# Inverting a triangular block with 32-wide instead of 64-wide tile products in a DeltaNet mixer

## The chip, the cores and the metric

The kernel runs on one core of one Trainium2 chip. The metric is the device time of one launch in microseconds (us), as the median of several runs. A core has five engines: TensorE (PE, matrix products; its weight loads are listed apart as PEld), VectorE (DVE), ScalarE (ACT), GpSimd (POOL) and SyncE (SP, which only issues transfers here). PE writes to the accumulation memory PSUM (8 banks of 128 partitions x 512 float32), the others take it from there.

## The reference, cut to what matters

One inference step of a two-layer backbone. Each layer has a mixer (windowed attention beside a bidirectional gated DeltaNet) and a routed mixture of experts. The change is in the DeltaNet's triangular solve:

```
a_mat = where(strict, einsum('bhnik,bhnjk->bhnij', kb, k) * decay, 0.0)
sol = triangular_solve(a_mat + eye(CHUNK), rhs, left_side=True, lower=True, unit_diagonal=True)
u0, w = sol[..., :DV], sol[..., DV:]
qk = where(causal, einsum('bhnik,bhnjk->bhnij', q, k) * decay, 0.0)
def step(S, xs):
    u = u0_c - einsum('bhck,bhkv->bhcv', w_c, S)
    o = einsum('bhck,bhkv->bhcv', qd_c, S) + einsum('bhij,bhjv->bhiv', qk_c, u)
    S = S * gt_c[..., None, None] + einsum('bhck,bhcv->bhkv', kd_c, u)
```

The kernel solves by an explicit inverse of `I + a_mat`, in chunks of 128 tokens. All of it is float32.

## The kernel before

The program has straight-line phases for each of two layers: projection, mixer, tail, experts, combine. Only the mixer phase (`mixer_phase`) changes. It runs 5 steps `s`, one per tile of 128 tokens, and in each step both directions `d` (0 forward, 1 backward) for 4 heads `h`. Every engine has its own instruction list, written out by hand; engines meet by semaphores alone, so the order within each list is the order of the code. Four attention pieces (`n0` to `n0 + 3`) are threaded between the DeltaNet's parts of a step: `next_scores` (PE: values of the piece before, then scores), `stats` (DVE: maximum), `exps` (ACT), `norm` (DVE), `turn` (PE: transposes), `take` (ACT: copy out of PSUM).

A step goes:

1. `g_p`, `r_p`: products K K^T and the decay exponents; ACT makes `E` (L1161), DVE makes `Bt` (two 64-wide diagonal blocks per 128, L1234) and `BtL` (the corner that joins them, L1236).
2. POOL masks `Bt` for each level into `NTb` (L964), DVE makes the first approximation `Y` (L1240), PE transposes it to `X` (L1052, copied by ACT L1168).
3. Five levels `v` (block sizes 2, 4, 8, 16, 32 are joined to pairs). In each, for both directions: `T1 = NTb^T X` (PE), a copy to SBUF (ACT, L1172), then `Y^T T1` and `T1^T Y` (PE), and DVE subtracts them from `X` (L1252) and `Y` (L1259). One product of all heads is `eight`: 8 matmuls with 64x64 tiles. In float32 each matmul is issued as two passes, and each pass is a weight load and a matmul record, so one `eight` is 32 PE records.
4. The last join of the two 64-blocks: `t1l` (L1104), ACT copies (L1179), `yl` (L1117), DVE copies into the inverse `YF` (L1274). Between them PE runs `ks`, and after them `turn(n0 + 1)` (L1022) and `qs` (L1045).
5. `z` on DVE (L1278, L1279), `next_scores(n0 + 2)` (L1034, L1001), then the solve `xz`, `u2`, state update, outputs and the last attention piece.

SP issues three small transfers at the mixer's start, and in layer 0 a fourth of 12.8 MB that fills `y_table` with zeros.

## Time and profile before

| | us |
|---|---|
| median of 3 runs (lowest, highest) | 2103.43 (2102.64, 2104.16) |
| the profiled execution's own time | 2101.1 |
| its span, first to last instruction | 2099.4 |
| PE / DVE / ACT / POOL busy | 1760.4 / 1294.8 / 958.4 / 211.8 |

The span is what the profiler saw of one execution. Busy time is a union over instructions of one engine; idle time in front of an instruction is listed with what released it. "issue" is idle time for which the profile shows no releaser. Times in a timeline count from the span's start. The mixer phase of layer 0 lies at 290 to 542 us, that of layer 1 at 1332 to 1573 us.

### The profile page before, as it was taken

The page shows a single profiled execution, that of the slowest core. Times are in us where ns is not written, and L with a number is a line of the kernel's source. Part 1 is how long each engine was busy: PE and PEld are TensorE (multiplying, and loading weights), DVE is VectorE, ACT ScalarE, POOL GpSimd, SP SyncE. Part 2 cuts the span into 40 slices and gives each one's busy share as a digit, 9 for nine tenths or more (in the row PEclk, how much of TensorE's full clock was granted, in tenths as well). Part 3 has the DMA queues.
Part 4 walks back from the last instruction along what each step waited for, and adds up shares of the span by engine and source line. Part 5 has one row for each costly group of instructions (what it writes and reads, how often), then busy time and mean ns, then how long its engine had stood idle before and what let it go on. Part 6 is the DMA issues. An engine that isn't in the chain of part 4 may idle for free. (4 is left out here: it accounts for less than half of the span.)

```text
span 2099.4 us, 38037 instructions
## 1 busy us (share of the span) xinstructions
PE 1760.4 (84%) x14245; PEld 1412.2 (67%) x14246; DVE 1294.8 (62%) x1877; ACT 958.4 (46%) x1486; POOL 211.8 (10%) x267
## 2 busy tenths in 40 slices
PE   5499978999698399999954999899987939999991
PEld 0299767888444188888843997788873538888881
DVE  0439635666443488696646495576662469999664
ACT  0134533343311288686633445343332238888641
POOL 0000022222000000000010000222220010000002
PEclk8699999999798599999986999999997969999995
DMA  9532043000557499798833220000004069999744
GB/s 393 238 110 79 5 147 128 3 2 2 172 218 274 192 387 399 283 392 339 300 144 111 87 83 1 13 12 2 3 2 143 31 228 389 407 397 397 311 171 180
DMA packets 96326, 376.48 MB, mean 179 GB/s; under 512 B 14478, under 2 KB 35030, under 8 KB 65478
## 3 DMA queue, kind: packets, MB, share of 16 engines
q1 hardware_dynamic: 80486, 316.76, 40.2%
q0 software_dynamic: 8496, 30.94, 3.9%
q10 hardware_dynamic: 7216, 26.97, 3.2%
q8 instruction: 94, 1.54, 0.3%
q14 instruction: 34, 0.28, 0.0%
HBM read 332.86 MB, written 41.78 MB: 178 GB/s over the span
## 5 line engine op out<-in xcount | busy, mean ns | idle before, releaser
L1926 DVE TENSOR_TENSOR expert_w_lo<-shared,expert_w_hi 128x2048 fp32r<-128x2048 f32 x192 | 430.5, 2284 | 44.0 <-ACT expert_w_hi L1868 42.9
L1868 ACT ACTIVATE expert_w_hi<-shared 128x2048 fp32r<-128x2048 f32 x192 | 361.3, 1916 | 56.2 <-PEq L142 52.0
L1810 PE MATMUL ps<-expert_w_hi,expert_x_hi 128*128 128x512 f32 x592 | 232.6, 393 | 5.1 <-DVE expert_x_lo L1922 5.1
L1812 PE MATMUL ps<-expert_w_hi,expert_x_lo 128*128 128x512 f32 x592 | 232.4, 393 | 0.0
L1811 PE MATMUL ps<-expert_w_lo,expert_x_hi 128*128 128x512 f32 x592 | 232.2, 392 | 0.0
L1810 PEld LDWEIGHTS ps<-expert_w_hi,expert_x_hi 128*128 128x128 f32 x592 | 112.4, 190 | 29.4 <-issue 5.9
L1811 PEld LDWEIGHTS ps<-expert_w_lo,expert_x_hi 128*128 128x128 f32 x592 | 112.3, 190 | 23.5
L1812 PEld LDWEIGHTS ps<-expert_w_hi,expert_x_lo 128*128 128x128 f32 x592 | 112.3, 190 | 23.5
L1846 PE MATMUL ps<-expert_w_hi,expert_hid_hi 128*128 128x512 f32 x296 | 118.6, 401 | 1.2 <-ACT expert_hid_hi L1900 0.5
L1847 PE MATMUL ps<-expert_w_lo,expert_hid_hi 128*128 128x512 f32 x296 | 115.6, 391 | 0.0
L964 POOL TENSOR_TENSOR mixer_NTb<-mixer_Bt,consts_sb 128x256 f32<-128x256 f32 x120 | 89.2, 767 | 229.2 <-DVE mixer_Bt L1234 181.1
L1409 PE MATMUL ps<-shared,attT 128*128 128x512 f32 x160 | 76.4, 625 | 28.9 <-DMA shared<-in_w_out 28.9
L603 PE MATMUL ps<-projection_hT_hi,kvrows_r 128*128 128x256 f32 (+1 forms) x384 | 90.3, 317 | 5.9 <-DVE shared_r L511 5.9
L1852 PE MATMUL ps<-expert_w_hi,expert_hid_lo 128*128 128x512 f32 x296 | 91.2, 389 | 0.0
L1252 DVE TENSOR_TENSOR mixer_X<-mixer_X,ps 128x256 f32<-128x256 f32 x100 | 42.2, 422 | 78.3 <-PE ps L1052 76.0
L607 PE MATMUL ps<-projection_hT_hi,shared_r 128*128 128x256 f32 (+1 forms) x384 | 88.6, 313 | 0.0
L565 PE MATMUL ps<-shared_r,projection_hT_hi 128*128 128x512 f32 (+1 forms) x240 | 88.2, 367 | 0.0
L771 DVE SCALAR_TENSOR_TENSOR shared<-shared,projection_cwT 128x644 f32<-128x644 f32 x96 | 85.2, 888 | 2.5
L1796 PE MATMUL ps<-consts_sb,expert_xg 128*128 128x128 f32 x312 | 54.9, 282 | 36.5 <-DMA expert_xg<-h_table,expert_cur_idx 36.5
L1172 ACT ACTIVATE mixer_T<-ps 128x256 f32<-128x256 f32 x100 | 38.4, 384 | 102.0 <-PE ps L1052 98.0
L1409 PEld LDWEIGHTS ps<-shared,attT 128*128 128x128 f32 x160 | 31.8, 201 | 68.9 <-issue 39.0
L1776 POOL COPY expert_cur_idx<-slot_tokens 128x1 int32 (+1 forms) x39 | 10.5, 270 | 647.9 <-PE ps L1796 588.8
(344 smaller groups left out, 3710.7 us busy)
## 6 DMA issues: line engine op xcount, KB each, us to landing
shared<-in_w_gate SPq DMA_DIRECT2D x64, 1024.0 KB, 6.8
shared<-in_w_up SPq DMA_DIRECT2D x64, 1024.0 KB, 8.6
shared<-in_w_down SPq DMA_DIRECT2D x64, 1024.0 KB, 18.8
setup_m_ada_ring<-in_w_ada SPq DMA_DIRECT2D x24, 1024.0 KB, 10.6
shared<-in_w_in SPq DMA_DIRECT2D x10, 2048.0 KB, 8.0
y_table<-expert_y ACTq DMA_DIRECT2D x37, 512.0 KB, 8.8
y_table<-zero SPq DMA_DIRECT2D x1, 12800.0 KB, 41.1
qkv<-in_w_ada SPq DMA_DIRECT2D x11, 1024.0 KB, 5.1
```

What stands on the lines that cost most here:

```text
L603: pe.matmul(out, w_hi[:, k, :], h_hi[:, k, t * P:until * P], start=(k == 0), stop=False)
L607: mm = pe.matmul(out, w_lo[:, k, :], h_hi[:, k, t * P:until * P], start=False, stop=(k == KD - 1))
L964: return pool.tensor_tensor(NTb[:, slot, d], Bt[:, d], row(G.c(f"level{level}_{d}"), DH), ALU.mult)
L1409: mm = pe.matmul(G.ps[:, BO + r % NOB, :], src[:, t * P:(t + 1) * P], wo[:, k, h * 512:(h + 1) * 512], start=(k == 0), stop=(k == KD - 1))
L1810: pe.matmul(bank, hi, w_hi[:, j, w], start=first, stop=False)
L1811: pe.matmul(bank, hi, w_lo[:, j, w], start=False, stop=False)
L1812: return pe.matmul(bank, lo, w_hi[:, j, w], start=False, stop=last)
L1846: pe.matmul(G.ps[:, 5 + h, :], h_hi[:, at], w_hi[:, j, w], start=(q == 0), stop=False)
L1847: pe.matmul(G.ps[:, 5 + h, :], h_hi[:, at], w_lo[:, j, w], start=False, stop=False)
L1852: mm = pe.matmul(G.ps[:, 5 + h, :], h_lo[:, at], w_hi[:, j, w], start=False, stop=(q == KF - 1))
L1868: act.activation(w_hi[:, j, :], raw[:, j, :], ACT.Copy).then_inc(w_hi_done, 1)
L1926: dve.tensor_tensor(w_lo[:, j, :], raw[:, j, :], w_hi[:, j, :].bitcast(F32), ALU.subtract).then_inc(w_lo_done, 1)
```

## The change

The blocks that the levels work on become 32 wide: four 32x32 diagonal tiles per head stand in a packed tile of 32 columns, `XY` holds `X` and `Y` side by side, and one product of all heads is `strips`, 16 matmuls with 32x32 tiles (64 PE records). `Bt` is kept whole (128 wide, one DVE instruction per direction), and the level's mask is no longer put on it by POOL: the product is made with the unmasked tile, and DVE multiplies the mask in when it copies `T1` out of PSUM. The first approximation is made by PE (`first_p`, four `strips`) and DVE. There are four levels. The join of 32-blocks to 64-blocks (`t2_p`, `merge_p`, `x64_done`, `y64_done`) and that of 64-blocks to the whole make only the corner block; ACT puts the pieces into `X64` and `YF`, DVE copies the diagonal into `YF`. `turn(n0 + 1)` and `next_scores` move behind both `qs`, `norm(n0 + 1)` behind `z`, `stats(n0 + 1)` behind the levels.

```diff
-LEVELS = [2, 4, 8, 16, 32]
+HB, QB = 64, 32
+LEVELS = [2, 4, 8, 16]
...
-        Bt, BtL = ph.sb("Bt", [P, 2, DH, HB]), ph.sb("BtL", [P, DH, HB])
...
+        Bt = ph.sb("Bt", [P, 2, DH, P])
+        XY = ph.sb("XY", [P, 2, 2, DH, QB])
+        T1 = ph.sb("T1", [P, 2, DH, QB])
+        X64 = ph.sb("X64", [P, DH, HB])
         T1L = ph.sb("T1L", [P, DH, HB])
-        NTb = ph.sb("NTb", [P, 2, 2, DH, HB])
...
-                def masked(slot, d, level):
-                    return pool.tensor_tensor(NTb[:, slot, d], Bt[:, d], row(G.c(f"level{level}_{d}"), DH), ALU.mult)
...
-                    for v in range(LV):
-                        for d in range(2):
...
-                            masked(v % 2, d, LEVELS[v]).then_inc(s_["nt_done"], 1)
...
-                def eight(b, c, lhsT, rhs, sem):
+                def strips(b, c, lhsT, rhs):
 
                     for h in range(DH):
-                        for r in range(2):
-                            mm = pe.matmul(G.ps[half(r), b, 256 * c + h * HB:256 * c + (h + 1) * HB],
-                                           lhsT(h)[half(r)], rhs(h)[half(r)], start=True, stop=True)
-                    mm.then_inc(s_[sem], 1)
+                        for q in range(4):
+                            mm = pe.matmul(G.ps[quarter(q), b, c + h * QB:c + (h + 1) * QB], lhsT(h, q), rhs(h, q), start=True, stop=True)
+                    return mm
...
+                    eye = lambda h, q: G.c("eye")[quarter(q)]
+                    for d in range(2):
+                        pe.wait_ge(s_["bt_done"], at(s, d))
+                        own = lambda h, q: Bt[quarter(q), d, h, quarter(q)]
+                        strips(d, 0, own, eye)
+                        strips(d, 128, eye, own).then_inc(s_["first_p"], 1)
+                    for d in range(2):
                         four(2 + d, kT[d], qT[d], "kq_p")
                     next_scores(n0)
-                    for d in range(2):
-                        pe.wait_ge(s_["y0_done"], at(s, d))
-                        eight(d, 0, lambda h: Y[:, d, h, :], lambda h: G.c("eye"), "x0_p")
                     for v in range(LV):
                         for d in range(2):
...
-                            eight(d, 0, lambda h: NTb[:, v % 2, d, h, :], lambda h: X[:, d, h, :], "t1_p")
+                            pe.wait_ge(s_["xy_done"], xy_at(s, v - 1, d))
+                            strips(d, 256, lambda h, q: Bt[quarter(q), d, h, quarter(q)],
+                                   lambda h, q: XY[quarter(q), d, 0, h, :]).then_inc(s_["t1_p"], 1)
                         if v == 2:
                             turn(n0)
                         if v == 3:
                             next_scores(n0 + 1)
                         for d in range(2):
                             pe.wait_ge(s_["t1_done"], lev(s, v, d))
...
-                            eight(d, 1, lambda h: Y[:, d, h, :], lambda h: T1[:, d, h, :], "xx_p")
-                            eight(2 + d, 0, lambda h: T1[:, d, h, :], lambda h: Y[:, d, h, :], "yy_p")
...
+                            y = lambda h, q: XY[quarter(q), d, 1, h, :]
+                            t1 = lambda h, q: T1[quarter(q), d, h, :]
+                            strips(d, 0, y, t1)
+                            strips(d, 128, t1, y).then_inc(s_["xy_p"], 1)
+                    for d in range(2):
+                        pe.wait_ge(s_["xy_done"], xy_at(s, LV - 1, d))
+                        for h in range(DH):
+                            for b in range(2):
+                                q1, q2 = halves_of(d, b)
+                                mm = pe.matmul(G.ps[quarter(q2), d, 256 + h * QB:256 + (h + 1) * QB], Bt[quarter(q1), d, h, quarter(q2)],
+                                               XY[quarter(q1), d, 0, h, :], start=True, stop=True)
+                        mm.then_inc(s_["t2_p"], 1)
+                    for d in range(2):
+                        pe.wait_ge(s_["t2_done"], at(s, d))
+                        for h in range(DH):
+                            q1, q2 = halves_of(d, d)
+                            pe.matmul(G.ps[quarter(q2), d, h * QB:(h + 1) * QB], XY[quarter(q2), d, 1, h, :], T1[quarter(q2), d, h, :],
+                                      start=True, stop=True)
+                            for b in range(2):
+                                q1, q2 = halves_of(d, b)
+                                mm = pe.matmul(G.ps[quarter(q1), d, 128 + h * QB:128 + (h + 1) * QB], T1[quarter(q2), d, h, :],
+                                               XY[quarter(q2), d, 1, h, :], start=True, stop=True)
+                        mm.then_inc(s_["merge_p"], 1)
+                    for d in range(2):
+                        pe.wait_ge(s_["qk_done"], at(s, d))
+                        pe.wait_ge(s_["x64_done"], at(s, d))
                     for h in range(DH):
                         for d in range(2):
-                            mm = pe.matmul(G.ps[half(1 - d), 2, h * HB:(h + 1) * HB], BtL[half(d), h, :],
-                                           X[half(d), d, h, :], start=True, stop=True)
+                            mm = pe.matmul(G.ps[half(1 - d), 2, h * HB:(h + 1) * HB], Bt[half(d), d, h, half(1 - d)],
+                                           X64[half(d), h, :], start=True, stop=True)
...
                     for d in range(2):
+                        pe.wait_ge(s_["y64_done"], at(s, d))
...
                     pe.wait_ge(s_["t1l_done"], s + 1)
...
-                    turn(n0 + 1)
                     four(2, qT[0], lambda h: S[:, st, 0, h, :], "qs_p")
                     pe.wait_ge(s_["yo_done"], s + 1)
                     four(3, qT[1], lambda h: S[:, st, 1, h, :], "qs_p")
+                    turn(n0 + 1)
...
+                    exps(n0)
+                    take(n0)
+                    for d in range(2):
+                        act.wait_ge(s_["t2_p"], at(s, d))
+                        act.activation(T1[:, d], t1_of(d), ACT.Copy).then_inc(s_["t2_done"], 1)
+                    for d in range(2):
+                        for q in (2 * d, 2 * d + 1):
...
+                            act.activation(X64[quarter(q), :, quarter(q % 2)], XY[quarter(q), d, 0], ACT.Copy)
+                    for d in range(2):
+                        act.wait_ge(s_["merge_p"], at(s, d))
+                        q1, q2 = halves_of(d, d)
+                        act.activation(X64[quarter(q2), :, quarter(q1 % 2)], pair_of(d)[quarter(q2), 0], ACT.Copy,
+                                       scale=-1.0).then_inc(s_["x64_done"], 1)
+                    for d in range(2):
+                        for b in range(2):
+                            q1, q2 = halves_of(d, b)
+                            ins = act.activation(YF[quarter(q1), d, :, quarter(q2)], pair_of(d)[quarter(q1), 1], ACT.Copy, scale=-1.0)
+                        ins.then_inc(s_["y64_done"], 1)
                     act.wait_ge(s_["t1l_p"], s + 1)
                     act.activation(flat(T1L[:, :, :]), G.ps[:, 2, 0:256], ACT.Copy, scale=-1.0).then_inc(s_["t1l_done"], 1)
-                    take(n0 + 1)
+                    exps(n0 + 1)
                     for d in range(2):
...
+                    take(n0 + 1)
...
-                        for b in range(2):
-                            ins = dve.tensor_tensor(Bt[half(b), d], bank(2 + d)[half(b), :, half(b)], E[half(b), d, :, half(b)], ALU.mult)
-                        ins.then_inc(s_["b_done"], 1)
...
-                    for d in range(2):
-                        dve.wait_ge(s_["n1_done"], at(s, d))
-                        dve.tensor_tensor(Y[:, d], NTb[:, 1, d], row(G.c("eye"), DH), ALU.add).then_inc(s_["y0_done"], 1)
+                        dve.tensor_tensor(Bt[:, d], bank(2 + d), E[:, d], ALU.mult).then_inc(s_["bt_done"], 1)
+                    for d in range(2):
+                        first = G.c(f"first_{d}").rearrange("p (a n) -> p a n", a=2).unsqueeze(2).to_broadcast([P, 2, DH, QB])
+                        dve.wait_ge(s_["first_p"], at(s, d))
+                        dve.tensor_tensor(XY[:, d], pair_of(d), first, ALU.mult).then_inc(s_["first_done"], 1)
+                        dve.wait_ge(s_["first_done"], at(s, d))
+                        both = XY[:, d].rearrange("p a h n -> p (a h) n")
+                        dve.tensor_tensor(both, both, row(G.c("eye"), 2 * DH), ALU.add).then_inc(s_["xy_done"], 1)
                     for d in range(2):
                         dve.wait_ge(s_["kq_p"], at(s, d))
                         dve.tensor_tensor(QK[:, d], bank(2 + d), E[:, d], ALU.mult).then_inc(s_["qk_done"], 1)
                     stats(n0)
                     for v in range(LV):
                         for d in range(2):
-                            dve.wait_ge(s_["xx_p"], lev(s, v, d))
...
-                            dve.tensor_tensor(X[:, d], X[:, d], blocks(d, 1), ALU.subtract).then_inc(s_["x_done"], 1)
...
+                            dve.wait_ge(s_["t1_p"], lev(s, v, d))
+                            dve.tensor_tensor(T1[:, d], t1_of(d), row(G.c(f"level{LEVELS[v]}_{d}"), DH), ALU.mult).then_inc(s_["t1_done"], 1)
+                        for d in range(2):
+                            dve.wait_ge(s_["xy_p"], lev(s, v, d))
+                            dve.tensor_tensor(XY[:, d], XY[:, d], pair_of(d), ALU.subtract).then_inc(s_["xy_done"], 1)
                         if v == 1:
                             norm(n0)
-                        if v == 3:
-                            stats(n0 + 1)
-                    norm(n0 + 1)
...
+                    for d in range(2):
+                        dve.wait_ge(s_["xy_done"], xy_at(s, LV - 1, d))
+                        for q in range(4):
+                            ins = dve.tensor_copy(YF[quarter(q), d, :, quarter(q)], XY[quarter(q), d, 1])
+                        ins.then_inc(s_["diag_done"], 1)
+                    stats(n0 + 1)
...
+                    norm(n0 + 1)
```

How the rows stand, in the third step of layer 0. PE, from the second level's first product on; `mixer_T_0` is `T1`. Before:

```order
L1052 MATMUL ps<-mixer_X,mixer_NTb 64x64 x16
L1052 MATMUL ps<-mixer_T_0,mixer_Y 64x64 x8
L1052 MATMUL ps<-mixer_Y,mixer_T_0 64x64 x8
L1052 MATMUL ps<-mixer_T_0,mixer_Y 64x64 x8
L1052 MATMUL ps<-mixer_Y,mixer_T_0 64x64 x8
L1052 MATMUL ps<-mixer_X,mixer_NTb 64x64 x16
L1022 MATMUL ps<-consts_sb,shared 128x128 x8
```

and now:

```order
L1057 MATMUL ps<-mixer_XY,mixer_Bt 32x32 x32
L1057 MATMUL ps<-mixer_T_0,mixer_XY 32x32 x16
L1057 MATMUL ps<-mixer_XY,mixer_T_0 32x32 x16
L1057 MATMUL ps<-mixer_T_0,mixer_XY 32x32 x16
L1057 MATMUL ps<-mixer_XY,mixer_T_0 32x32 x16
L1057 MATMUL ps<-mixer_XY,mixer_Bt 32x32 x32
L1027 MATMUL ps<-consts_sb,shared 128x128 x8
```

Each product has twice the matmuls; the place of the transposes (`turn(n0)`) is the same.

PE from the corner's first product on, before:

```order
L1104 MATMUL ps<-mixer_X,mixer_BtL 64x64 x8
L1045 MATMUL ps<-shared,qkvT 128x128 x8
L1117 MATMUL ps<-shared,mixer_T1L 64x64 x8
L1022 MATMUL ps<-consts_sb,shared 128x128 x8
L1045 MATMUL ps<-shared,qkvT 128x128 x8
L1034 MATMUL ps<-shared,qkv 64x128 x6
L1034 MATMUL ps<-shared,mixer_vctx 64x128 x2
```

and now:

```order
L1125 MATMUL ps<-mixer_X_0,mixer_Bt 64x64 x8
L1050 MATMUL ps<-shared,qkvT 128x128 x8
L1139 MATMUL ps<-shared,mixer_T1L 64x64 x8
L1050 MATMUL ps<-shared,qkvT 128x128 x8
L1027 MATMUL ps<-consts_sb,shared 128x128 x8
L1039 MATMUL ps<-shared,qkv 64x128 x6
L1039 MATMUL ps<-shared,mixer_vctx 64x128 x2
```

The transposes of piece `n0 + 1` stand directly ahead of the values that need them.

DVE from the last subtraction of a level on, before (L1221 to L1224 are `norm(n0 + 1)`, L1278 and L1279 make `z`):

```order
L1264 TENSOR_TENSOR shared<-mixer_Y,ps 64x4x64 x2
L1221 TENSOR_TENSOR mixer_rden<-mixer_rsum,mixer_es 128x2
L1222 RECIPROCAL mixer_rden<-mixer_rden 128x2
L1224 TENSOR_SCALAR shared<-shared,mixer_rden 128x512 x2
L1274 COPY shared<-ps 64x4x64 x2
L1278 TENSOR_TENSOR shared<-ps,dn_ecum 128x512
L1279 TENSOR_TENSOR shared<-kvrows,shared 128x512
L1278 TENSOR_TENSOR shared<-ps,dn_ecum 128x512
L1279 TENSOR_TENSOR shared<-kvrows,shared 128x512
```

and now (L1252 to L1255 are `norm(n0 + 1)`):

```order
L1247 TENSOR_TENSOR mixer_sx<-mixer_nm,mixer_sink 128x2
L1295 COPY shared<-ps 64x4x64 x2
L1299 TENSOR_TENSOR shared<-ps,dn_ecum 128x512
L1300 TENSOR_TENSOR shared<-kvrows,shared 128x512
L1299 TENSOR_TENSOR shared<-ps,dn_ecum 128x512
L1300 TENSOR_TENSOR shared<-kvrows,shared 128x512
L1252 TENSOR_TENSOR mixer_rden<-mixer_rsum,mixer_es 128x2
L1253 RECIPROCAL mixer_rden<-mixer_rden 128x2
L1255 TENSOR_SCALAR shared<-shared,mixer_rden 128x512 x2
```

`norm(n0 + 1)` stood ahead of the copies into `YF` and now stands behind all of `z`.

## Rows read from the trace of the kernel before

**Rows 1.** The page: span, instruction fetch queue of PE (packets, MB, share), one transfer.

```profile
span 2099.4 us, 38037 instructions
...
q8 instruction: 94, 1.54, 0.3%
...
y_table<-zero SPq DMA_DIRECT2D x1, 12800.0 KB, 41.1
```

**Rows 2.** Busy time in both mixer phases: window, length, engines (x records), PEclk, DMA.

```profile
290.00:541.80 251.80, 220.13 (x3904) 197.40 (x3904) 163.46 (x379) 92.70 (x274) 64.09 (x77) 1.00 0.18 59
1331.50:1572.60 241.10, 219.29 (x3904) 196.93 (x3904) 162.23 (x377) 92.67 (x274) 64.06 (x77) 1.00 0.03 7
```

**Rows 3.** Timeline, third step of layer 0, one level: start, length, engine, line.

```profile
403.71 0.85 ACT L1172 ACTIVATE mixer_T<-ps 128x256 f32<-128x256 f32 x2 [0.75 <-PE ps L1052]
...
404.14 0.68 PE L1052 MATMUL ps<-mixer_T,mixer_Y 64*64 64x64 f32 x16
...
406.74 0.85 ACT L1172 ACTIVATE mixer_T<-ps 128x256 f32<-128x256 f32 x2 [2.18 <-PE ps L1052]
```

**Rows 4.** Timeline, the same step from `E` to the solve's first product.

```profile
391.45 2.25 ACT L1161 ACTIVATE shared<-ps,dn_bias 128x128 f32<-128x128 f32 x8 [0.24 <-PE ps L1070]
...
400.68 0.85 ACT L1172 ACTIVATE mixer_T<-ps 128x256 f32<-128x256 f32 x2 [0.40 <-PE ps L1052]
...
420.98 0.68 PE L1104 MATMUL ps<-mixer_X,mixer_BtL 64*64 64x64 f32 x16 [0.77 <-DVE mixer_X L1252]
...
422.11 0.88 DVE L1224 TENSOR_SCALAR shared<-shared,mixer_rden 128x512 f32<-128x512 f32 x2
...
423.57 0.68 PE L1117 MATMUL ps<-shared,mixer_T1L 64*64 64x64 f32 x16
424.18 0.85 PEld L1022 LDWEIGHTS ps<-consts_sb,shared 128*128 128x128 f32 x8
...
425.32 1.02 ACT L1154 ACTIVATE shared<-ps 128x1024 f32<-128x1024 f32 x1 [3.22 <-PE ps L1022]
...
429.27 1.86 PEld L1045 LDWEIGHTS ps<-shared 128*128 128x128 f32 x16
```

**Rows 5.** Timeline of PE, first step of layer 0, two of four idle gaps.

```profile
307.62 0.39 PE L1052 MATMUL ps<-mixer_X,mixer_NTb 64*64 64x64 f32 x6 [2.73 <-issue]
...
328.50 0.50 PE L1104 MATMUL ps<-mixer_X,mixer_BtL 64*64 64x64 f32 x9 [2.26 <-issue]
```

**Rows 6.** Windows from gap to gap there; columns as in rows 2.

```profile
307.60:314.50 6.90, 4.41 (x125) 4.02 (x126) 3.62 (x9) 1.54 (x4) 4.13 (x5) 1.00 1.06 357
314.50:321.30 6.80, 4.58 (x125) 4.14 (x125) 2.10 (x5) 0.77 (x2) 0.00 (x0) 1.00 1.05 351
```

**Rows 7.** Transfers: at 304.5 to 332 us, at 353.9 to 357.7 us, and the smallest.

```profile
q8 instruction: 4, 0.07, 0.9%
q8 instruction: 2, 0.03, 3.4%
mixer_sink<-in_sink SPq DMA_DIRECT2D x1, 4.0 KB, 2.2
```

**Rows 8.** DVE groups by form: busy, mean ns of one, idle before.

```profile
L1252 DVE TENSOR_TENSOR mixer_X<-mixer_X,ps 128x256 f32<-128x256 f32 x100 | 42.2, 422 | 78.3 <-PE ps L1052 76.0 <-issue 0.3
L1213 DVE TENSOR_REDUCE mixer_mx<-ps 128x2 f32<-128x1024 f32 x16 | 19.5, 1222 | 10.5 <-PE ps L1011 10.5
L1243 DVE TENSOR_TENSOR shared<-ps,shared 128x512 f32<-128x512 f32 x20 | 12.9, 686 | 0.3
L1202 DVE COPY attT<-ps 128x128 f32<-128x128 f32 x40 | 11.4, 285 | 10.9 <-PE ps L1034 10.4
```

**Rows 9.** The smallest matmuls, in layer 0's tail.

```profile
685.46 0.27 PE L1482 MATMUL ps<-ones_bf,tail_sel 128*16 128x1 bf16 x5 [6.88 <-DVE tail_sel L1660]
```

**Rows 10.** Setup, before and after PE's clock fell; columns as in rows 2.

```profile
19.70:23.00 3.30, 1.28 (x12) 0.16 (x8) 0.00 (x0) 0.00 (x0) 0.00 (x0) 1.00 1.01 422
23.00:29.80 6.80, 5.54 (x24) 0.60 (x24) 1.38 (x2) 0.00 (x0) 0.00 (x0) 0.50 1.01 419
```

More of the change, by code:

```diff
@@ L77, in constants, with joined @@
     parts = {"ident": j == i, "ones": np.ones((P, P)), "upper": j <= i, "lower": j >= i, "before": j < i}
-    ib = HB * (j // HB) + np.arange(HB)[None, :]
-    parts["eye"] = j == ib
-    for s in [1] + LEVELS:
-        sign = -1.0 if s == 1 else 1.0
-        same = (j // (2 * s)) == (ib // (2 * s))
-        parts[f"level{s}_0"] = sign * (same & (j % (2 * s) < s) & (ib % (2 * s) >= s))
-        parts[f"level{s}_1"] = sign * (same & (j % (2 * s) >= s) & (ib % (2 * s) < s))
+    iq = QB * (j // QB) + np.arange(QB)[None, :]
+    parts["eye"] = j == iq
+    def joined(s):
+        same = (j // (2 * s)) == (iq // (2 * s))
+        below = same & (j % (2 * s) >= s) & (iq % (2 * s) < s)
+        above = same & (j % (2 * s) < s) & (iq % (2 * s) >= s)
+        return below, above
+    below, above = joined(1)
+    parts["first_0"] = -1.0 * np.concatenate([below, above], axis=1)
+    parts["first_1"] = -1.0 * np.concatenate([above, below], axis=1)
+    for s in LEVELS:
+        parts[f"level{s}_0"], parts[f"level{s}_1"] = joined(s)
     parts["tokens"] = np.stack([np.broadcast_to(np.arange(NT)[None, :] * P, (P, NT)),
@@ L921, in at, with lev, xy_at, halves_of @@
             return 2 * s + d + 1
-        def lev(s, v, d, n=LV):
-            return 2 * (n * s + v) + d + 1
+        def lev(s, v, d):
+            return 2 * (LV * s + v) + d + 1
+        def xy_at(s, v, d):
+            return 2 * ((LV + 1) * s + v + 1) + d + 1
+        def halves_of(d, b):
+            return (2 * b, 2 * b + 1) if d == 0 else (2 * b + 1, 2 * b)
         def first_visit(s, d):
@@ L940, in mixer_phase @@
         half = lambda b: slice(HB * b, HB * (b + 1))
+        quarter = lambda q: slice(QB * q, QB * (q + 1))
+        pair_of = lambda d: G.ps[:, d, 0:256].rearrange("p (a h n) -> p a h n", a=2, h=DH)
+        t1_of = lambda d: G.ps[:, d, 256:384].rearrange("p (h n) -> p h n", h=DH)
         bank = lambda b: G.ps[:, b, :].rearrange("p (h n) -> p h n", h=DH)
@@ L1254, in _ @@
-                            if v:
-                                dve.wait_ge(s_["y_done"], lev(s, v - 1, d, LV - 1))
-                            else:
-                                dve.wait_ge(s_["y0_done"], at(s, d))
-                            if v < LV - 1:
-                                dve.tensor_tensor(Y[:, d], Y[:, d], blocks(2 + d), ALU.subtract).then_inc(s_["y_done"], 1)
-                            else:
-                                if s == 0:
-                                    dve.wait_ge(s_["yf_zero"], 1)
-                                for b in range(2):
-                                    ins = dve.tensor_tensor(YF[half(b), d, :, half(b)], Y[half(b), d], blocks(2 + d)[half(b)],
-                                                            ALU.subtract)
-                                ins.then_inc(s_["yf_done"], 1)
+                            dve.wait_ge(s_["t1_p"], lev(s, v, d))
```

51 lines of the change are left out of this document (8 added, 43 removed).

## The prediction

> **What bounds the kernel now.** I read the two mixer windows first: they take 251.8 and 241.1 us of the span of 2099.4, TensorE's clock is at its full level throughout (share 1.00, which is 2.4 GHz), PE is busy 220 of them, DVE 163, ACT 93, POOL 64 [rows 1, 2]. Nothing outside the mixers changes, so the question is ten steps (five per layer), about 50 us each. Then I followed the third step of layer 0 in the timeline. One level takes 3.03 us (the copies of `T1` start at 403.71 and 406.74) [rows 3]. The 16 passes of one `eight` take 0.68 us with the last one's latency of 0.22, so 0.46 without; six of these are 2.8 of the 3.03: inside the levels PE's products are the bound. From `E` (391.45) to the first copy of `T1` (400.68) it is 9.2 us, from there to the corner product 20.3 (420.98), from the second corner product `yl` (423.57) to the solve `xz` (429.27) 5.7 [rows 4]. Layer 0's first step has something else: PE stands idle until 307.62 and 328.50, the first and last of four such gaps, without a releaser [rows 5], and from one resumption to the next there are 125 or 126 matmuls and as many weight loads [rows 6]. With the semaphore instructions that is 256 records, and four packets of 16 KB were fetched in that time (4 for 27.5 us) [rows 7]: 16 KB is 256 instructions of 64 bytes. So PE's instructions come in blocks of 256, at most one block is fetched ahead, and while the 12.8 MB of zeros (41.1 us to landing) [rows 1] hold the queues at a DMA share of 1.06, one block takes 6.9 us [rows 6].
>
> **What the change does to the products.** An `eight` was 32 PE records, a `strips` is 64. Per step 32 `eight` (1,024 records) become 28 `strips` and two small joins (1,792 + 160 = 1,952): about 930 more on some 1,650. How long does a `strips` take? In an `eight` two tiles alternate and 16 passes take 0.46 us, 29 ns each, 58 ns per pass on one tile [rows 3]. With half the columns and four tiles, 32 passes take 8 x 29 = 0.23 us if tiles are independent; if each pass costs what tiny matmuls on one tile do ((0.27 - 0.165) / 4 = 26 ns [rows 9]; 0.165 is the latency of one), 0.83 us. I take 0.27: the existing products show tiles overlapping, and the 26 ns row uses a single tile.
>
> The Trainium skill ("TensorE: Matmul & The Clock Gate", Back-to-back issue gap) gives a floor of about 25 ns per matmul however small; the tiny row agrees. By that rule a `strips` would be 32 x 25 = 0.8 us; it is the second rival.
>
> **Levels without a supply limit.** One direction's chain: `t1` 0.27 + 0.2 latency, hand-over 0.05, DVE masks 128 columns (0.29, the 128-column copy from PSUM [rows 8]), hand-over 0.05, two `strips` 0.54 + 0.2, 0.05, DVE subtracts 256 columns 0.42 [rows 8], 0.05: 2.1 us per level against 3.03. The other direction fits in between. `norm(n0)` puts 1.4 on DVE ahead of the third level's masks, `turn(n0)` 0.9 on PE, the scores 2.3 in the fourth; in all 12.5 us for four levels. The join adds `t2`, ACT's copies and the merge. ACT's 128-column instructions follow each other every 0.28 us (8 in 2.25 [rows 4]), and eight of them (two `T1`, four diagonal copies, two corners) are in the chain: 2.5 us. The corner product starts 15.05 us after the first `T1` copy instead of 20.3.
>
> **Head.** `Bt` takes one DVE instruction of 0.69 [rows 8] instead of three of 0.42; four `strips` are done while `E`'s second half is made; the first masks of `T1` now stand on DVE behind `stats(n0)` (reduce 1.22 [rows 8], and 0.6 around it). The first copy comes at 400.95 instead of 400.68: +0.3. POOL's masks cost nothing before (hidden) and nothing after.
>
> **Supply.** From there the third step needs 1,640 records to the end of the merge, 6.4 blocks, and 384 per level, 1.5 blocks in 2.1 us: one per 1.4 us. How long is one block's fetch L without the zeros? The smallest transfer, 4 KB, lands after 2.2 us; a fetch of 16 KB runs in one packet of 1.07 us on average (0.3% of 16 x 2099 us for 94 packets) [rows 1, 7]. Below: 2.2. Above: 3.6, since two packets 3.6 us apart were followed by no idle time [rows 7]. I take 2.2 + 1.07 less the small transfer's own part of some 0.35 = 2.9. Walking the step: a block is entered at 401.25 and the next arrives L later, four times in a row, since their contents last less than L; then the scores (56 records in 2.3 us) space the next entry by 3.65; the last block waits L again; ACT's last copies add 1.1. The corner product stands at 401.25 + 4L + 3.65 + L + 1.1 = 406.0 + 5L = 420.5 for L = 2.9, against 420.98 before. Nearly all that the levels won is lost waiting for instructions: -0.5 (with the head in it).
>
> **Tail.** Before, `norm(n0 + 1)` ran at 422.11 beside `ks`, the transposes at 424.18, ACT's `take` at 425.32, the values from 427, `xz` at 429.27 [rows 4]. Now the norm stands behind the `YF` copies (0.86) and four `z` instructions (2.75). Counted from `yl`: 0.7 until it is out, 0.86, 2.75, norm 1.3, transposes to `take` 1.15, `take` 1.0, hand-over 0.1, values and scores 2.3: `xz` follows 10.15 us after `yl` instead of 5.7. The queue behind the waiting transposes is values, scores and the solve itself, for which the DeltaNet's own `z` has long been ready. +4.45 per step. In the first step of a layer the pieces are narrower and I take +3.5.
>
> **Layer 0's first step.** From the first products until 331.7, when the zeros have landed, blocks come every 6.9 to 7 us. The block boundary 165 records into the phase is passed at about 296.3, the next block is there at 304.5, then 311.5, 318.5, 325.4, 331.7; then L apart: 334.6, 337.5. The step needs about 2,090 records up to the end of the merge, which lies in the last of these: 338.4, corner product 339.3 instead of 328.5 [rows 5]. +10.8, and the tail's 3.5: +14.3.
>
> **Sum.** Nine steps x (-0.5 + 4.45) = +35.6, the first step +14.3: +50 us. On the profiled execution's own 2101.1 (span 2099.4 and 1.7 around it) that is 2151; the median of the runs is 2.3 above the profiled execution, so 2153.
>
> **Rivals.**
> - *Supply never binds without the zeros, or at all* (other side: faster). Place: the block boundaries in the levels. If L is under 1.4 us, the third step's corner comes at 416.0 (-5.0) and the tail gives back 4.45: -0.5 per step. If layer 0's first step is not held up either, 10 x -0.5 = -5: 2098. For it: in 9 of 10 steps the trace shows no such gap. Against: rows 5 and 6, and the 2.2 us of the smallest transfer. If only the first step is held, 9 x -0.5 + 13 = +8: 2111. What decides between faster and not is whether a block arrives in the 1.4 us in which its forerunner is used up.
> - *Passes are bound by issue*, 26 ns each: a level is six times 0.83 = 5.0 us, the four with norm, turn and scores some 23, the head +1.1; corner +4.6, tail +4.45, 9 us in ten steps: +90, 2193.
> - *The clock falls too.* In the setup PE was busy 1.28 of 3.3 us at share 1.00 and then stood at 0.50 (1.2 GHz) in the 6.8 us behind it [rows 10]. In the levels it would have six `strips` of 0.27 in some 4.3 us. At half clock turn, scores and part of `ks` take twice as long, about 4 us per step: +90, 2190. Against: the mixer of before kept its clock over gaps of 2.7 us.
>
> The Trainium skill ("Runtime: NRT & Kernel Launch", Instruction fetch mechanics) says that code comes in 16 KB blocks, which rows 6 and 7 bear out, but also that PE holds 2,048 instructions and that fetching is hidden because issue is slower. By that rule the first rival holds and the time would be 2098; gaps exactly 256 records apart speak against such a store.
>
> **How the numbers follow.** A difference under 0.2% (4 us) can't be told from none. Forecast, supply-bound levels at full clock: 0.52. The clock falls too: 0.13. Issue-bound: 0.08. Only the first step held (2111): 0.11. Supply never binds: 0.16; its 2098 is so near the bound that 0.07 of it is within 0.2%. So faster 0.09, same 0.07, slower 0.84. L = 2.2 gives +0.5 per step and 2120, L = 3.6 gives +7.5 and 2188 (first step +17). The range of 8 in 10 goes from the case with one held step, 2108, to 2190.
>
> **What would show it.** Right: matmuls with 32x32 tiles in groups of 32 passes within 0.3 us and a latency; idle time of PE put down to "issue" of 1 to 2 us in most levels, 256 records apart, PE's fetch queue at about 130 packets instead of 94; the corner product of the third step 29 us after `E` as before; between `qs` and the transposes an idle gap of PE of about 3 us, ended by DVE's norm; the first step of layer 0 longer by over 10 us. Wrong: levels of 2.1 us without such gaps (then the tail alone decides, near 2100), passes 26 ns apart, or the clock share under 1 in the mixer windows.

## The result and the profile after

The changed kernel takes 2236.21 us (median of 4 runs, 2231.62 to 2237.60), the kernel before 2103.03 (2100.96 to 2104.16): a ratio of 1.0631, interval 1.0618 to 1.0643, slower by 133 us. The forecast was 2153 in a range of 2108 to 2190. The direction was right and the size was not: 50 us were forecast.

The page of the kernel after, against [rows 1], and the two mixer phases, against [rows 2] (columns: window, length, busy us of PE, PEld, DVE, ACT, POOL, then granted clock as a share, DMA share, GB/s):

```profile
span 2235.9 us, 46814 instructions
...
q8 instruction: 130, 2.13, 0.4%
```

```profile
290.00:604.50 314.50, 232.16 (x6194) 201.22 (x6195) 144.71 (x370) 85.34 (x269) 19.36 (x18) 0.79 0.14 48
1404.00:1703.00 299.00, 231.42 (x6193) 200.48 (x6194) 144.52 (x370) 85.15 (x269) 19.27 (x18) 0.80 0.02 7
```

Four things stand here. The mixers are 314.5 and 299.0 us long instead of 251.8 and 241.1. PE's busy time grew by 12 us only (232 for 220), so most of the added time is time in which PE waits. The clock share is 0.79 and 0.80 instead of 1.00. And PE's fetches went from 94 packets to 130, as forecast.

The waits of PE in layer 0's mixer (waiting line, releaser, us in total, times, longest):

```profile
PE ps L1057 <- issue: 38.2, 18, 4.6
PE ps L1027 <- DVE shared L1255: 18.7, 10, 4.5
PE ps L1125 <- ACT mixer_X L1201: 6.6, 5, 1.4
PE ps L1039 <- ACT shared L1176: 4.5, 5, 1.1
```

The first is a wait for nothing that the profile shows, in the 32x32 products. The third step's timeline places it:

```profile
431.18 0.45 PE L1057 MATMUL ps<-mixer_T,mixer_XY 32*32 32x32 f32 x32 [1.23 <-DVE mixer_T L1279]
...
433.32 0.32 PE L1057 MATMUL ps<-mixer_T,mixer_XY 32*32 32x32 f32 x14
...
435.26 0.47 PE L1057 MATMUL ps<-mixer_T,mixer_XY 32*32 32x32 f32 x17 [1.61 <-issue]
...
435.55 0.60 PE L1057 MATMUL ps<-mixer_XY,mixer_T 32*32 32x32 f32 x28
...
438.72 0.95 PE L1057 MATMUL ps<-mixer_XY,mixer_Bt 32*32 32x32 f32 x50 [1.53 <-issue]
```

```profile
435.26:438.72 3.46, 1.93 (x128) 1.79 (x128) 1.96 (x6) 0.00 (x0) 0.00 (x0) 0.50 0.02 5
```

PE stops in the middle of a `strips`, after 14 of its 32 passes, and from one resumption to the next there are 128 matmuls and 128 weight loads, one block of 256, in 3.46 us. That is the L of the forecast, which took 2.9. The other steps agree: all ten have such stops, 39 in all. Sixteen pairs of neighbouring stops outside the zeros are one block of 256 records apart and 3.46 to 4.01 us apart (mean 3.67, most often 3.46 or 3.75); in layer 0's first step, under the zeros, four pairs are 6.2 us apart.

The same step, the rows that answer to [rows 4], and the clock behind the levels:

```profile
421.23 2.25 ACT L1183 ACTIVATE shared<-ps,dn_bias 128x128 f32<-128x128 f32 x8 [0.24 <-PE ps L1074]
...
430.84 0.48 DVE L1279 TENSOR_TENSOR mixer_T<-ps,consts_sb 128x128 f32<-128x128 f32 x2
...
453.37 1.12 PE L1125 MATMUL ps<-mixer_X,mixer_Bt 64*64 64x64 f32 x16 [1.36 <-ACT mixer_X L1201]
454.41 3.78 PE L1050 MATMUL ps<-shared,qkvT 128*128 128x128 f32 x16
458.12 1.01 PE L1139 MATMUL ps<-shared,mixer_T1L 64*64 64x64 f32 x16
459.06 2.19 PE L1050 MATMUL ps<-shared,qkvT 128*128 128x128 f32 x16
464.06 1.09 PE L1027 MATMUL ps<-consts_sb,shared 128*128 128x128 f32 x8 [2.81 <-DVE shared L1255]
466.27 1.55 PE L1039 MATMUL ps<-shared,qkv 128*64 128x128 f32 x12 [1.11 <-ACT shared L1176]
...
470.58 2.94 PE L1050 MATMUL ps<-shared 128*128 128x128 f32 x16
```

```profile
452.10:458.90 6.80, 5.53 (x46) 5.22 (x48) 2.08 (x6) 4.07 (x14) 0.00 (x0) 0.50 0.01 2
458.90:465.70 6.80, 3.45 (x32) 2.89 (x28) 4.64 (x10) 2.69 (x9) 0.00 (x0) 1.00 0.00 0
465.70:472.50 6.80, 6.23 (x37) 5.08 (x38) 1.84 (x4) 0.53 (x2) 0.00 (x0) 0.50 0.00 0
```

Two groups of 16 passes on 128x128 tiles start 4.65 us apart: `ks` takes 3.78 us, `qs` 2.19. The windows name the difference: the clock is at 0.50 (1.2 GHz) for the first and at 1.00 (2.4 GHz) for the second. PE then waits for the norm (2.81 us) and for ACT (1.11 us), and in the stretch behind that the share is 0.50 again, for values, scores and part of `xz`.

With the same five marks in all ten steps of both profiles (first instruction of each, weight loads included; in a layer's last step the state's update stands for the next `E`), the time splits so:

| stretch, sum of ten steps | before | after | forecast | measured |
|---|---|---|---|---|
| `E` to first `T1` | 85.6 | 91.2 | +2.7 | +5.6 |
| `T1` to corner product | 199.7 | 243.0 | +3.6 | +43.3 |
| corner to `yl` | 28.4 | 43.8 | 0 | +15.4 |
| `yl` to `u2` (the first read of `xz`) | 66.9 | 133.0 | +43.6 | +66.1 |
| `u2` to next `E` | 88.6 | 90.7 | 0 | +2.1 |

(Forecast: nine times +0.3, -0.8 and +4.45; the first step's +10.8 stands in the second row and +3.5 in the fourth.)

### The profile page after: what moved, and what is told of

It reads as the page before. It is cut to its first block and busy times, and to the rows that moved or that the text cites. A ratio compares the mean times of both kernels' runs of the same rounds, so it can differ in the third digit from the quotient of the medians.

```text
span 2235.9 us, 46814 instructions
## 1 busy us (share of the span) xinstructions
PE 1786.6 (80%) x18885; PEld 1421.2 (64%) x18886; DVE 1265.7 (57%) x1877; ACT 946.6 (42%) x1486; POOL 123.0 (6%) x149
## 5 line engine op out<-in xcount | busy, mean ns | idle before, releaser
L1176 ACT ACTIVATE shared<-ps 128x768 f32<-128x768 f32 (+2 forms) x40 | 32.6, 815 | 159.6 <-PE ps L1027 159.6
L1282 DVE TENSOR_TENSOR mixer_XY<-mixer_XY,ps 128x256 f32<-128x256 f32 x80 | 33.7, 422 | 113.6 <-PE ps L1057 111.8
L1874 PE MATMUL ps<-expert_w_hi,expert_hid_lo 128*128 128x512 f32 x296 | 91.2, 389 | 0.0
L1027 PE MATMUL ps<-consts_sb,shared 128*128 128x128 f32 x240 | 44.5, 334 | 45.9 <-DVE shared L1255 45.7
L1431 PE MATMUL ps<-shared,qkvT 128*128 128x512 f32 x160 | 76.7, 624 | 0.0
L610 PEld LDWEIGHTS ps<-projection_hT_hi,kvrows_r 128*128 128x128 f32 x384 | 70.2, 192 | 8.6 <-DVE shared_r L518 8.5
```

The costliest lines, as they stand in the source:

```text
L610: pe.matmul(out, w_hi[:, k, :], h_hi[:, k, t * P:until * P], start=(k == 0), stop=False)
L1431: mm = pe.matmul(G.ps[:, BO + r % NOB, :], src[:, t * P:(t + 1) * P], wo[:, k, h * 512:(h + 1) * 512], start=(k == 0), stop=(k == KD - 1))
L1874: mm = pe.matmul(G.ps[:, 5 + h, :], h_lo[:, at], w_hi[:, j, w], start=False, stop=(q == KF - 1))
```

## The experiments

Times are medians, ratios are against the kernel before on the same chip.

**The order at the step's end, both ways.** In the changed kernel it was put back, in the kernel before it was put in:

```diff
 # PE: turn(n0 + 1) ahead of qs        (and the reverse in the kernel before)
+turn(n0 + 1)
 four(2, qT[0], ..., "qs_p")
 ...
-turn(n0 + 1)
 # ACT: take(n0 + 1) ahead of the oz copies; DVE: norm(n0 + 1) ahead of the YF copies
```

> The changed kernel with the order at the step's end as it was before: norm(n0+1) ahead of the YF copies, turn(n0+1) ahead of qs, take(n0+1) ahead of the oz copies; nothing else. Changed kernel 2236.2. Theory (the prediction's tail term stands): at full clock the order is worth 4.45 us per step, and as measured in the changed kernel's third step (12.46 us from yl to xz against 5.70 before) up to 6.8, since part of it runs at half clock: 2168 to 2192, and xz follows yl within 6 to 8 us. Rival (the wait only moves: exps(n0+1) comes late because stats(n0+1) now stands behind the levels, or PE waits for instructions there too): 0 to -15, 2221 to 2236.

> The kernel before (64-column blocks) with only the changed kernel's order at the step's end: norm(n0+1) behind z, turn(n0+1) behind qs, take(n0+1) behind the oz copies. Before 2103.0. Theory: +4.45 us in nine steps, +3.5 to 4.5 in the first of each layer, clock share still 1.00: 2145 to 2149. If the new gap of PE also takes the clock to its half for the values and scores: another 1 to 2.5 per step, up to 2172. Rival (the gap is hidden by z, which waits for ks anyway): under +10, 2103 to 2113.

Put back: 2175.74 us (1.0343, 1.0326 to 1.0361), 60.5 less than the changed kernel; `yl` to `u2` sums to 69.3 instead of 133.0. Alone in the kernel before: 2168.16 us (1.0309, 1.0292 to 1.0326), 65 more, and that stretch sums to 132.8. So nearly half of the change's loss is this reordering, whatever the block size. Both lie within what was expected, and the second only with the half clock in it. In the kernel before with the moved order, third step:

```profile
440.64 1.97 PE L1022 MATMUL ps<-consts_sb,shared 128*128 128x128 f32 x8 [2.81 <-DVE shared L1224]
442.64 1.02 ACT L1154 ACTIVATE shared<-ps 128x1024 f32<-128x1024 f32 x1 [3.63 <-PE ps L1022]
443.72 1.55 PE L1034 MATMUL ps<-shared,qkv 128*64 128x128 f32 x12 [1.11 <-ACT shared L1154]
```

The gap of 2.81 us is the forecast's; what follows it runs at half clock (share 0.50 from 440.0 to 446.8 us), here too, although the 64-column levels ahead of it had kept it full.

**Filling that gap.** Three matmuls of 512 columns go into the gap, their results thrown away:

```diff
 four(3, qT[1], ..., "qs_p")
+for _ in range(3):
+    pe.matmul(G.ps[:, 7, :], G.c("ident"), flat(QK[:, 0]), start=True, stop=True)
 turn(n0 + 1)
```

> The kernel before with the moved order of the step's end (as in the run that measured 2168.2) and three added matmuls (128x128 by 128x512, f32, into an idle PSUM bank, results thrown away) in PE's new gap between qs and the transposes. Theory (the gap costs twice: the wait itself, about 4.45 us, and the half clock that follows it through transposes, values and scores, about 2): the filled gap keeps the clock full, from yl to u2 12 us instead of 14.2 to 15.9, in all 2145 to 2152. Rival (the moved order's whole +6.5 is waiting, the half clock costs nothing): 2168 or more.

Measured 2150.91 us (1.0233, 1.0216 to 1.0250), 17 less for more work. The same place:

```profile
433.87 2.74 PE L1124 MATMUL ps<-shared,consts_sb 128*128 128x512 f32 x6
...
436.84 1.09 PE L1022 MATMUL ps<-consts_sb,shared 128*128 128x128 f32 x8 [0.23 <-DVE shared L1226]
437.97 1.02 ACT L1156 ACTIVATE shared<-ps 128x1024 f32<-128x1024 f32 x1 [2.75 <-PE ps L1022]
439.05 0.88 PE L1034 MATMUL ps<-shared,qkv 128*64 128x128 f32 x12 [1.11 <-ACT shared L1156]
```

The transposes take 1.09 us instead of 1.97, the values' first group 0.88 instead of 1.55. The windows around both places, without and with the added matmuls, have the clock share at 0.79 and 1.00:

```profile
433.00:449.00 16.00, 12.08 (x102) 10.25 (x98) 6.33 (x14) 3.58 (x10) 0.00 (x0) 0.79 0.00 1
```

```profile
430.00:446.00 16.00, 14.09 (x118) 10.89 (x116) 8.81 (x21) 5.71 (x16) 0.00 (x0) 1.00 0.00 1
```

From `yl` to `u2` it is 11.88 us in this step against 7.49 before: +4.39, where the forecast had +4.45. The term was right at full clock; the half clock was missing beside it. In the fourth step of each layer the stretch took longer, 15.0 and 13.4 us. In layer 0 the clock fell all the same (0.50 from 496.5 to 499.9 us). In layer 1 it stayed full, and the norm itself came later:

```profile
1546.72 2.94 POOL L990 TENSOR_TENSOR shared<-shared,o 128x512 f32<-128x512 f32 x2 [16.05 <-ACT shared L1185]
1547.36 1.17 DVE L1280 TENSOR_TENSOR shared<-kvrows,shared 128x512 f32<-128x512 f32 x1
1548.46 1.22 DVE L1223 TENSOR_TENSOR mixer_rden<-mixer_rsum,mixer_es 128x2 f32<-128x2 f32 x1
```

While POOL adds the outputs of the other direction, DVE's last `z` instruction takes 1.17 us instead of 0.69 and the norm's first 1.22 instead of 0.15. The changed kernel and the kernel with the moved order show the same in the fourth and fifth step of each layer, and in no other step. In the filled kernel these steps cost +5.94 (layer 1's fourth) and +5.22 us over the kernel before instead of +4.39. No run took POOL's work away, so the cause is read from the coincidence alone.

**Is it the supply in the levels?** One kernel issues the products of `T1` twice, one makes the levels' products for two heads only (the other two heads' inversion is left out):

```diff
-strips(d, 256, own_bt, x).then_inc(s_["t1_p"], 1)
+for _ in range(2):
+    mm = strips(d, 256, own_bt, x)
+mm.then_inc(s_["t1_p"], 1)
```

```diff
-for h in range(DH):        # in the levels' strips alone
+for h in range(2):
```

> The changed kernel with the 16 products of T1 issued twice in every level (same operands, same place; +512 records per step, 2 blocks of 256). Changed kernel 2236.2. Theory (a block of 256 records arrives every 3.5 us in the levels): +7.0 us per step, 2306, with q8 at 150 packets and the gaps of PE still 256 records apart. Rival (PE's own time bounds): four levels x two directions x 0.27 to 0.42 us = +2.2 to 3.4 per step, 2258 to 2270.

> The changed kernel with the products of the four levels made for two of the four heads only (768 records per step fewer, 3 blocks of 256; the other two heads' inversion is left out, while DVE's instructions keep their size). Changed kernel 2236.2, from the first T1 to the corner 22.5 us in the third step. Theory (supply, 3.5 us per block): -10.5 us per step until the dependency chain takes over, which the prediction put at 15 us from the first T1 to the corner; so 14 to 16 us there, -7 to -8 per step and more in layer 0's first: 2145 to 2170. Rival (PE's own time): half of 24 strips of 0.27 us saved, -3.3 per step, 2203. Rival (the hand-overs between PE and DVE bound): hardly less than before, above 2215.

Doubled: 2312.98 us (1.1005, 1.0987 to 1.1023), +76.8 for 20 more blocks, 3.8 us each. Two heads: 2136.24 us (1.0152, 1.0131 to 1.0172), -100.0 for 30 blocks fewer, 3.3 us each; the best case had been put at 2145, so this fell below the expected range. The fetch packets, doubled and then with two heads:

```profile
q8 instruction: 150, 2.46, 0.5%
```

```profile
q8 instruction: 100, 1.64, 0.3%
```

The issue waits of the products in layer 0's mixer:

```profile
PE ps L1057 <- issue: 57.9, 29, 4.3
```

```profile
PE ps L1063 <- issue: 8.2, 3, 3.4
```

29 stops with the doubled products, 18 in the changed kernel, 3 with two heads. In the third step of the last the corner product follows the first `T1` after 15.57 us, and the forecast's chain without a supply limit had 15.05. That agreement is looser than it looks. With two heads the forecast's chain would be some 1.6 us shorter (half of twelve `strips` of 0.27), and the clock share was 0.78 in the stretch. What the run does show is that the supply no longer binds: the 3 stops all stand in layer 0's first step, under the zeros, and the nine others have none longer than 0.25 us. Records added and records taken away move the time by 3.3 to 3.8 us per block, and PE's own time, the rival, is out by a factor of two or more both ways. The clock share of layer 0's mixer is 0.80 with two heads as well, and corner to `yl` sums to 45.7: the clock falls without the supply's stops too.

**Half clock: cause or sign?** Two added matmuls per level in the changed kernel; then the same with the old order at the step's end and three more around the join (in both, the first level's fill also waits for `QK`):

```diff
 # behind the T1 products, behind the products of X and Y
+pe.matmul(G.ps[:, 2 + d, :], G.c("ident"), flat(QK[:, d]), start=True, stop=True)
```

> The changed kernel with two added matmuls per level (128x128 by 128x512, f32, into the two PSUM banks that lie idle there; 8 records and about 1.7 us of PE work per level, both results thrown away), to keep TensorE's activity up while it waits. Changed kernel 2236.2. Theory (levels are bound by the supply of instructions, 3.5 us per block of 256 records, and the half clock costs time behind the levels): the added work fits in the gaps and costs only its 32 records, +0.4 to +0.9 per step; the clock stays full in the levels and ks runs in 2.1 instead of 3.8 us: in all -1 to -2.5 per step, 2211 to 2226. Rival 1 (half clock is only a sign of waiting and costs nothing): +4 to +9, 2240 to 2245. Rival 2 (PE's own work bounds the levels): +6.8 per step, 2300.

> The changed kernel with the old order at the step's end (that run: 2175.7) and added matmuls (f32, 128x512 columns, thrown away): two per level, three around the join. Theory (ks runs at half clock because PE waited in the join just before; 4.8 us from corner to yl against 2.6 before): the fills keep the clock full, corner to yl back to 2.6 (-2.2 per step), against +1 to +2 per step for the fills' own records and work: 2163 to 2176. Rival (ks is slow for another reason than the clock, such as waiting for the YF copies): corner to yl stays near 4.8, 2186 to 2196.

Fills in the levels alone: 2246.27 us (1.0682, 1.0664 to 1.0700), +10, where rival 1 had said up to +9. The clock rose only to 0.89 and 0.92 in the mixers: it still fell at the join in eight of the ten steps, and `T1` to corner grew by 12.6 us in the sum. So this kernel doesn't tell the two apart behind the levels; inside them, a fuller clock bought nothing that can be seen. Fills around the join as well: 2181.31 us (1.0368, 1.0351 to 1.0386), 5.6 more than the kernel with the old order alone, a little above the 2163 to 2176 expected; but the disputed stretch answers clearly. Its third step:

```profile
444.26 1.98 PE L1054 MATMUL ps<-shared,consts_sb 128*128 128x512 f32 x4
446.17 0.68 PE L1136 MATMUL ps<-mixer_X,mixer_Bt 64*64 64x64 f32 x16
446.79 2.05 PE L1050 MATMUL ps<-shared,qkvT 128*128 128x128 f32 x16
448.77 0.68 PE L1150 MATMUL ps<-shared,mixer_T1L 64*64 64x64 f32 x16
```

```profile
290.00:575.00 285.00, 250.51 (x6295) 185.78 (x6294) 141.32 (x371) 83.55 (x268) 18.88 (x18) 0.97 0.16 53
```

`ks` is back at 2.05 us and corner to `yl` at 2.59 in all ten steps (25.9 instead of 46.1 in the kernel without fills). The 2.2 us are the clock's. What lets it fall is PE's wait around the join, as far as these two kernels show: fills in the levels alone left the stretch at 39.2 (43.8 without), and the fills around the join came on top of them, with the old order. The fills lost more than that elsewhere, by delaying products and by their own records (+22.6 from `T1` to corner).

**One part of the change alone, on 64-column blocks.** The corner-only join takes the place of the last level in the kernel before; the attention's pieces stand one level earlier:

```diff
-LEVELS = [2, 4, 8, 16, 32]
+LEVELS = [2, 4, 8, 16]
+# behind the levels: t2 = Bt[q1, q2]^T X[q1]; corner of X = -(Y[q2]^T t2); corners of YF = -(t2^T Y[q2])
+# PE, ACT copy, PE, ACT copies with scale -1, as in the changed kernel
```

> The kernel before with one idea of the change alone: its last level (joining 32-row blocks on 64-column packs) makes the corner block only, with the changed kernel's join; norm, transposes and scores of the attention stand one level earlier, everything else as before. Before 2103.0. Theory (PE's time in the levels bounds, supply does not with 192 records per level): the last level's 3.0 us and its subtractions give way to a join of about 2.1: -1 per step, 2093 (2087 to 2098). Rival (the join's chain of PE, ACT, PE, ACT leaves PE waiting 1.4 us and the clock falls for ks, +2.2): 2103 to 2118.

Measured 2091.43 us (0.9937, 0.9920 to 0.9953): within the 2087 to 2098 of the theory, and 0.6% faster than the kernel before. Third step of layer 1, from the last level's subtraction to the corner product:

```profile
1444.01 0.41 DVE L1297 TENSOR_TENSOR mixer_X<-mixer_X,ps 128x256 f32<-128x256 f32 x1
...
1444.19 0.73 PE L1112 MATMUL ps<-mixer_X,mixer_Bt 32*32 32x32 f32 x32
...
1444.89 0.44 ACT L1208 ACTIVATE mixer_T<-ps 128x128 f32<-128x128 f32 x2
...
1445.72 0.56 ACT L1214 ACTIVATE mixer_X<-ps 32x128 f32<-32x128 f32 x2 [0.39 <-PE ps L1124]
...
1446.42 0.68 PE L1130 MATMUL ps<-mixer_X,mixer_BtL 64*64 64x64 f32 x16 [0.56 <-ACT mixer_X L1214]
```

2.4 us from the start of that subtraction; first `T1` to corner is 18.64 us against 20.31. In the third and fourth step of layer 0 the clock fell behind the join and took 1.6 us of it back, and layer 0's first step, under the zeros, gained nothing (51.2 us against 50.4).

**The zeros.** The 12.8 MB go out in five pieces, each at a step's corner product, in the kernel before, in the changed one and in the one with the join:

```diff
-sp.dma_start(dst, zeros).then_inc(G.y_zero, 16)
+for s in range(NT):
+    sp.wait_ge(s_["t1l_done"], s + 1)
+    sp.dma_start(dst[:, cuts[s]:cuts[s + 1]], zeros_of(s)).then_inc(G.y_zero, 16)
+sp.wait_ge(G.y_zero, 16 * NT)
```

> The kernel before with the 12.8 MB of zeros of layer 0 not sent at the mixer's start but in five pieces, one at each step's corner product. Before 2103.3. Theory (the zeros lengthen the fetch of PE's instructions to 6.9 us per block, which stalls only where PE uses more than a block in that time, in the levels): layer 0's first step falls from 50.4 to 41 to 43 us, the pieces of some 8 us end before the next levels: 2094 to 2098. Rival (each step's fetches are delayed instead by its piece): 2100 to 2106.

> The changed kernel with the zeros in five pieces, one at each step's corner product. Changed kernel 2236.2; its first step takes 68.0 us in layer 0 and 54.8 in layer 1. Theory (the difference is the zeros' hold on the fetches): the first step falls to 55 to 57, 2222 to 2228. Rival (the pieces stall the later steps instead): 2232 to 2240.

> The kernel before with the 64-column levels, the corner-only last join (that run: 2091.4) and the zeros in five pieces at the corner products. Theory (the two gains add): layer 0's first step falls from 51.2 to 40 to 42: 2080 to 2086. Rival (the zeros' pieces cost the later steps what the first gains): 2088 to 2094.

Before: 2094.22 us (0.9957, 0.9943 to 0.9970), layer 0's first step 41.07 us instead of 50.42, the same as layer 1's. Changed: 2223.25 us (1.0567, 1.0552 to 1.0582), first step 54.5 instead of 68.0. With the join: 2075.93 us (0.9878, 0.9862 to 0.9893), below the 2080 to 2086 expected and 6 us more than the sum of the two gains. About 3 of these are the clock's, which was full throughout; about 2 are the first step's, 39.5 us, where the join now gains as it does in layer 1:

```profile
290.00:515.00 225.00, 205.46 (x3777) 183.88 (x3778) 154.00 (x378) 96.43 (x298) 56.96 (x67) 1.00 0.20 66
1310.00:1540.00 230.00, 208.10 (x3794) 185.64 (x3794) 157.47 (x384) 96.58 (x298) 56.95 (x67) 1.00 0.03 7
```

> The same (64-column levels, corner-only last join, zeros in pieces) with two added matmuls in PE's waits of the join (f32, 128 and 256 columns, results thrown away). Theory (the half clock behind the join, which cost 1.6 us from corner to yl in some steps of the join's own run, comes from those waits): corner to yl 2.6 in all steps, -2 to -5 beside the kernel without them. Rival (the fills delay the join, or the clock falls elsewhere): 0 to +6.

2078.94 us (0.9885, 0.9870 to 0.9900): no better, the rival's case, and 3 us from the kernel without them, which is within the spread of the runs. The clock was full without the fills. Why it fell in two steps of the join's first kernel and not here was not settled.

## Why the prediction was wrong in size

Three steps of the prediction failed. It took 2.9 us for the fetch of a block, where 3.46 to 3.75 were measured. It priced every step's levels with the third step's. And it took the clock to stay full, where it fell in every step (17 to 41 us of each at half clock). Its account of the supply and of the waiting norm held.

- *What bounds the kernel now*: right. Where records were taken away the levels shrank, and where the order was put back the step's end did.
- *Records and fetches*: right, 130 packets. *A `strips` takes 0.27 us*: right; 32 passes lie within 0.45 us with the last one's latency of 0.19 at full clock. The second rival (26 ns per pass) falls with it: 8 ns each where four tiles take turns. The row that the 26 ns came from [rows 9] ran on one tile and at clock share 0.50. The Trainium skill's floor of about 25 ns per matmul ("TensorE: Matmul & The Clock Gate", Back-to-back issue gap) does not hold for such tiles; the trace decides.
- *L = 2.9 us*: the first term mis-sized. Measured 3.46 in the trace, 3.3 and 3.8 from the blocks taken away and added. The forecast's own formula with 3.5 gives +2.2 us for the third step's stretch from `T1` to corner (22.5), and 22.50 was measured (the steps outside the zeros took 22.2 to 23.8). Nine steps x 5 x 0.6 are 27 us; with the mean of 3.67 it would be 35. The bound above, 3.6, had been read off two packets 3.6 us apart with no stop behind them [rows 7], and ten of the sixteen pairs of stops are further apart than that; the smallest transfer's 2.2 us was the wrong row to lean to.
- *All steps priced with the third*: second error. The supply time does not shrink with the attention's narrower pieces, the levels of before did: 17.3 us in layer 1's first step, 19.1 to 19.5 in the second and the last, 20.3 in the third [rows 4]. Taking those five steps at 20.3 hid 7 us. With the two, 34 of the 39.7 us that the stretch has over the forecast are explained, and with the mean of 3.67 nothing is left over (42).
- *Tail +4.45 per step*: right at full clock, +4.39 measured in the third step. It left out that DVE's instructions ahead of the norm get slower beside POOL in the fourth and fifth steps.
- *Layer 0's first step*: +14.3 forecast, +17.6 measured. That its levels came out at +10.7 for 10.8 is luck. The forecast counted from 328.50, where PE resumes in the middle of the corner product; the product's first pass stands at 325.80. It also had blocks 6.9 to 7 us apart, where they came every 6.2, and the first stop (303.00, 2.64 us) fell ahead of the first `T1`, outside this row. From `E` to the corner product's first pass the step grew by 13.1 us.
- *The clock stays full*: this step failed in its mechanism. The rival had the place and the price (4 us per step, 0.13) and was argued down with the gaps of 2.7 us that the kernel before survives [rows 5]. That argument did not carry: in the kernel before with the moved order a single wait of 2.81 us was followed by the half clock. Why the gaps of [rows 5] were not is not shown. The changed kernel has several stops in a row, the join's wait of 1.4, and the norm's wait of 2.8; with two heads it has no stops outside layer 0's first step and the clock falls all the same. Its price: 15.4 us at `ks` by the table (20.2 by the filled kernel) and 18.9 behind the norm (132.8 against 113.9), together 3.4 us per step or a little more. The rival alone, 2190, was too low because it kept L = 2.9.
- *The rivals on the other side*: out. The supply binds in every step. The Trainium skill's statement ("Runtime: NRT & Kernel Launch", Instruction fetch mechanics) that fetching is hidden because issue is slower does not hold here: 20 more blocks cost 76.8 us. The Trainium skill's block of 16 KB (same section) does hold, 36 packets more for some 9,000 more records.

- *What would show it*: the stops 256 records apart, the 130 packets, the gap between `qs` and the transposes (2.81 us) and the first step came as said; the corner product 29 us after `E` did not (32.1), and the clock share under 1, named as a sign against the forecast, did come.

Sum: 50 forecast, 27 for L, 7 for the steps priced alike, 34 for the clock: 118 of 133. The other 15 lie in the levels (5.7, gone if L is taken at 3.67), in the first stretch (2.9, of which 2.4 are the first stop under the zeros), behind `yl` (3.6, about the size of what the four steps beside POOL cost, 4.8 by the filled kernel) and in small pieces that no run isolated.

## What to carry to other kernels

Count instruction records as a resource of their own: once products get so small that 256 records are used up faster than a block of them arrives (3.5 us here), cutting the arithmetic further only makes PE wait, and every other edit is priced against that wait. Price each new idle stretch of PE twice, for its length and for the large matmuls behind it at half clock. And test the parts of a change apart: here the join alone gained 0.6%, the new order at the step's end alone lost 3.1%, the change without that order lost 3.4%, and the whole change lost 6.3%.

## What the runs showed of the hardware

- Passes on four 32x32 tiles in turn start 8 ns apart at full clock and 13 at half (32 in 0.45 us and 28 in 0.60, latencies 0.19 and 0.24 taken off).
- A fetch of PE's instructions competes with data: under the zeros a block took 6.9 us [rows 6] in the kernel before and 6.2 in the changed one, and moving these away gave 8.4 us in the kernel before and 13.0 in the changed one. The time from block to block in the levels (3.5 us) is three times the 1.07 us that a fetch's packet takes on average [rows 1].
- More work can be faster: three thrown-away matmuls in a gap of 2.8 us saved 17 us over the ten steps, and the clock share went from 0.79 to 1.00 there. In the levels and the join the same means cost more than it gave.
- DVE's instructions took longer while POOL was at work: 1.17 to 1.38 us instead of 0.69 for a subtraction of 128x512, 1.21 instead of 0.15 for an addition of 128x2.
